# All weight sums of the seven-product windows on VectorE, from plain loads

## The reference

```python
h = h + 0.5 * swiglu(rmsnorm(h, ffn1_norm), w_gate, w_up, w_down)
h = h + mixer(h)                      # retention and differential attention
h = h + 0.5 * swiglu(rmsnorm(h, ffn2_norm), w_gate, w_up, w_down)

def swiglu(x, w_gate, w_up, w_down):
    return (jax.nn.silu(x @ w_gate) * (x @ w_up)) @ w_down
```

## Time and profile before

| | us |
|---|---|
| median of 3 runs | 3177.53 |
| profiled execution | 3177.6 |
| its span, first to last instruction | 3175.9 |
| PE busy | 3056.9 (96%) |
| DVE busy | 2021.3 (64%) |
| ACT busy | 1436.5 (45%) |
| POOL busy | 172.2 (5%) |
| the four stages of windows, about | 4 x 190 |

### The profile page before, as it was taken

The page is one execution under the profiler, slowest core; times in us unless marked ns, Lnnn a source line. Parts: engine busy times, 40 slices in busy tenths (PEclk is TensorE's granted clock), DMA queues, the critical chain, the costliest instruction groups (busy, mean ns, idle before and its releaser), DMA issues.

```text
span 3175.9 us, 55413 instructions
## 1 busy us (share of the span) xinstructions
PE 3056.9 (96%) x20248; PEld 2764.3 (87%) x20248; DVE 2021.3 (64%) x2999; ACT 1436.5 (45%) x2472; POOL 172.2 (5%) x209
## 2 busy tenths in 40 slices
PE   8999998999999899999999999999999999999997
PEld 6778785787887689999899999999999989879986
DVE  4445545773576478855566788647885566768854
ACT  3444433663343255533652455425553365246641
POOL 1000000000000011100000011001110000001100
PEclk9999999999999899999999999999999999999998
DMA  4111232222222247532121377325753212247622
GB/s 154 61 54 60 93 100 87 91 94 93 93 92 93 79 128 184 149 102 91 60 68 54 105 192 179 97 98 150 180 151 100 87 60 68 66 130 187 170 100 99
DMA packets 121787, 341.22 MB, mean 107 GB/s; under 512 B 13774, under 2 KB 13774, under 8 KB 121536
## 3 DMA queue, kind: packets, MB, share of 16 engines
q1 hardware_dynamic: 96768, 290.50, 27.2%
q0 software_dynamic: 23600, 46.87, 8.8%
q10 hardware_dynamic: 1296, 2.14, 0.2%
HBM read 337.29 MB, written 2.17 MB: 107 GB/s over the span
## 4 chain that ended last, share of the span: by engine, by line
PE 66%; issue 24%; DVE 4%; ACT 3%; DMA 2%; DVEq 1%; POOL 1%; ACTq 0%; POOLq 0%; SPq 0%
PE ps L2009 28%; PE ps L2070 9%; PE ps L2300 7%; PE ps L2303 7%; PE ps L2301 7%; PE ps L2585 3%; DMA s_raw<-in_stream 2%; PE ps L2084 1%; DVE rstd L1217 1%; PE ps L2366 1%; PE ps L2152 1%; ACT w_hi L673 1%; ACT f L875 1%; DVE w_lo L1212 1%; DVE h_lo L1223 0%
## 5 line engine op out<-in xcount | busy, mean ns | idle before, releaser
L673 ACT ACTIVATE w_hi<-w_raw 128x1024 fp32r<-128x1024 f32 x352 | 372.7, 1059 | 833.8 <-PE ps L2009 587.4
L1212 DVE TENSOR_TENSOR w_lo<-w_raw,w_hi 128x1024 fp32r<-128x1024 f32 x360 | 440.3, 1223 | 484.6 <-ACT w_hi L673 476.1
L2009 PE MATMUL ps<-f_hi,w_hi 128*128 128x264 f32 (+1 forms) x1488 | 385.7, 317 | 2.0 <-DVE f_lo L1489 2.0
L2009 PE MATMUL ps<-f_lo,w_hi 128*128 128x264 f32 (+1 forms) x1488 | 385.2, 317 | 0.0
L2009 PE MATMUL ps<-f_hi,w_lo 128*128 128x264 f32 (+1 forms) x1488 | 385.1, 316 | 0.0
L2009 PE MATMUL ps<-h_hi,w_hi 128*128 128x512 f32 (+1 forms) x896 | 303.0, 367 | 42.1 <-DVE h_lo L1223 28.5
L2009 PE MATMUL ps<-h_lo,w_hi 128*128 128x512 f32 (+1 forms) x896 | 295.8, 359 | 0.0
L2009 PE MATMUL ps<-h_hi,w_lo 128*128 128x512 f32 (+1 forms) x896 | 294.3, 358 | 0.0
L2009 PEld LDWEIGHTS ps<-f_hi,w_hi 128*128 128x128 f32 x1488 | 244.4, 188 | 22.2 <-issue 2.9
L2009 PEld LDWEIGHTS ps<-f_lo,w_hi 128*128 128x128 f32 x1488 | 245.7, 189 | 19.7
L2009 PEld LDWEIGHTS ps<-f_hi,w_lo 128*128 128x128 f32 x1488 | 245.2, 188 | 19.7
(11 more groups left out here) (365 smaller groups left out, 7489.0 us busy)
## 6 DMA issues: line engine op xcount, KB each, us to landing
w_raw<-in_stream SPq DMA_DIRECT2D x436, 512.0 KB, 3.3
s_raw<-in_stream SPq DMA_DIRECT2D x152, 256.0 KB, 4.9
s_raw<-in_stream POOLq DMA_DIRECT2D x152, 256.0 KB, 4.7
tmp<-in_stream SPq DMA_DIRECT2D x76, 256.0 KB, 5.4
xT<-in_x ACTq DMA_DIRECT2D x8, 256.0 KB, 9.7
xT<-in_x POOLq DMA_DIRECT2D x1, 2048.0 KB, 8.7
out<-tmp SPq DMA_DIRECT2D x8, 256.0 KB, 2.1
const<-in_const POOLq DMA_DIRECT2D x1, 1636.0 KB, 9.2
```

The lines of the kernel that those rows point to most:

```text
L673: nc.scalar.activation(w_hi[:, s, :], w_raw[:, s, :], ACT.Copy).then_inc(hi_done, 1)
L1212: V.tensor_tensor(w_lo[:, s, :], w_raw[:, s, :], w_hi[:, s, :].bitcast(F32), ALU.subtract).then_inc(lo_done, 1)
L2009: last = T.matmul(out[:, p, :], w[:, s, j * P:(j + 1) * P], x[:, k, c0:c1], start=start and j == 0 and r == 0, stop=stop and j == len(ks) ...
```

## The change

SyncE loads w21 (not w22) into s1_raw and no longer loads s3_raw. GpSimd issues no accumulating transfers. DVE's `sums` computes all four sums: s3 from w21 and w11, a drain, s1 in place from w21 and w22 (in tmp), a drain, and s2 and s4 as before. ScalarE waits for DVE's s1 (a new semaphore `s1_sum`) ahead of s1 upper, and no longer waits ahead of s3 upper.

```diff
@@ win_load (SyncE)
-                sp.dma_start(s1_raw[:, q, :], up[:, BLK:]).then_inc(s1_base[q], 16)
-                if not first:
-                    sp.wait_ge(win_lo, 6 * (E - 2) + LO["s3"])
-                sp.dma_start(s3_raw[:, q, :], gate[:, 0:BLK]).then_inc(s3_base[q], 16)
+                sp.dma_start(s1_raw[:, q, :], up[:, 0:BLK]).then_inc(s1_base[q], 16)
@@ GpSimd
-            def win_add(which, L, e, i, q):
-                unit = 2 * (ffn2_base(which, L)[0] + PLAIN + e)
-                w21 = stream_d[at(unit + 1), :, 0:BLK].rearrange("a p n -> (a p) n")
-                pool.wait_ge(s1_base[q], landed(which, L, i, q))
-                pool.sem_inc(carried, 1)
-                pool.dma_start(s1_raw[:, q, :], w21, accum_op=ALU.add).then_inc(s1_in[q], 16)
-                pool.wait_ge(s3_base[q], landed(which, L, i, q))
-                pool.sem_inc(carried, 1)
-                pool.dma_start(s3_raw[:, q, :], w21, accum_op=ALU.add).then_inc(s3_in[q], 16)
...
-                ffn2_sums(0, L)
...
-                ffn2_sums(1, L)
@@ ScalarE
-                def s1_upper(i, q):
-                    act.wait_ge(s1_in[q], landed(which, L, i, q))
+                def s1_upper(E, q):
+                    act.wait_ge(s1_sum, E + 1)
                     nc.scalar.activation(wx_hi[:, 0, :], s1_raw[:, q, :], ACT.Copy).then_inc(win_hi, 1)
...
                 def s3_upper(i, q):
-                    act.wait_ge(s3_in[q], landed(which, L, i, q))
                     nc.scalar.activation(wx_hi[:, 2, :], s3_raw[:, q, :], ACT.Copy).then_inc(win_hi, 1)
@@ VectorE
                 def sums(i, q):
-                    dve.wait_ge(s1_in[q], landed(which, L, i, q))
+                    dve.wait_ge(s1_base[q], landed(which, L, i, q))
                     dve.wait_ge(wg_in[q], landed(which, L, i, q))
+                    dve.wait_ge(w22_in[q], landed(which, L, i, q))
+                    V.tensor_tensor(s3_raw[:, q, :], s1_raw[:, q, :], w_raw[:, q, 0:BLK], ALU.add)
+                    dve.drain()
+                    V.tensor_tensor(s1_raw[:, q, :], s1_raw[:, q, :], tmp[:, 2 + q, 0:BLK], ALU.add).then_inc(s1_sum, 1)
+                    dve.drain()
                     V.tensor_tensor(s2_raw, s1_raw[:, q, :], w_raw[:, q, 0:BLK], ALU.add)
                     dve.drain()
                     V.tensor_tensor(s4_raw, s2_raw, w_raw[:, q, BLK:], ALU.add).then_inc(win_sum, 1)
```

More of the change, by code:

```diff
@@ L294, in program @@
         wg_in, w22_in = [sem("wg_in0"), sem("wg_in1")], [sem("w22_in0"), sem("w22_in1")]
-        s1_base, s1_in = [sem("s1_base0"), sem("s1_base1")], [sem("s1_in0"), sem("s1_in1")]
-        s3_base, s3_in = [sem("s3_base0"), sem("s3_base1")], [sem("s3_in0"), sem("s3_in1")]
+        s1_base = [sem("s1_base0"), sem("s1_base1")]
+        s1_sum = sem("s1_sum")
         win_sum, win_hi, win_lo = sem("win_sum"), sem("win_hi"), sem("win_lo")
@@ L634, in inverse_root @@
                 nc.gpsimd.tensor_tensor(out, out, power[0:out.shape[0], 0:out.shape[1]], ALU.pow).then_inc(done, 1)
-            def win_add(which, L, e, i, q):
-                unit = 2 * (ffn2_base(which, L)[0] + PLAIN + e)
-                w21 = stream_d[at(unit + 1), :, 0:BLK].rearrange("a p n -> (a p) n")
-                pool.wait_ge(s1_base[q], landed(which, L, i, q))
-                pool.sem_inc(carried, 1)
-                pool.dma_start(s1_raw[:, q, :], w21, accum_op=ALU.add).then_inc(s1_in[q], 16)
-                pool.wait_ge(s3_base[q], landed(which, L, i, q))
-                pool.sem_inc(carried, 1)
-                pool.dma_start(s3_raw[:, q, :], w21, accum_op=ALU.add).then_inc(s3_in[q], 16)
-            def ffn2_sums(which, L):
-                win_pairs(pool, lambda e, i, q: win_add(which, L, e, i, q))
-                win_add(which, L, N_WIN - 1, N_WIN // 2, 0)
             for L in range(LAYERS):
-                ffn2_sums(0, L)
                 for k in (0, 1, "m", 2, 3):
@@ L938, in win_pair @@
                     copy_out(by, 3, -1.0)
-                    s1_upper(ni, nq)
+                    s1_upper(E + 1, nq)
                     after(E, "w11")
@@ L996, in ffn2 @@
                 split_hi(*following(u0 + 1, 1))
-                s1_upper(0, 0)
+                s1_upper(E0, 0)
                 act.wait_ge(unit_done, 2 * u0 + 5)
```

## The result

| | before | after |
|---|---|---|
| median, us | 3177.53 | 3193.1 (3191.54 to 3193.62) |
| ratio to before, with its 95% interval | | 1.0053 [1.0038, 1.0067] |
| profiled execution, and its span | 3177.6, 3175.9 | 3193.1, 3191.3 |

The kernel became slower: the medians are 15.6 us apart (0.49%), and the ratio, taken of the means of five runs each, is 1.0053. The forecast was 3200 with a range from 3187 to 3215. So the direction is right, and 7 us of the size are missing. The trace says where.

A forecast was written before the change was run, and what follows sets the result against it. PE set the pace before, and DVE was to become the bound of the window stages. Stage terms of +4.1, +4.6, +6.0 and +7.7 gave +22.4 us on 3177.6, so 3200.0 us, range 3187 to 3215.

The forecast's parts named there:

- DVE's cycle: Window stages: 8.92 us without waits, plus 1.54 for two drained additions and 0.04 for a wait, 10.50 (fourth stage 10.44).
- DVE becomes the bound: Window stages: DVE's 10.50 us cycle passes PE's 10.18, by 0.32 us per window and more in the fourth stage.
- How PE feels it: In most windows PE waits about 0.3 us before its s2 product, because ACT's copy stands behind DVE's s1.
- The gap of 1.67 ahead of the first window: First stage's start: PE's gap of about 2 us goes, since DVE no longer waits for the accumulation.
- Entry: Stage starts: first sum 3.45 us after plain_up, then 18 cycles to the last window, 189.0 us (fourth stage 187.9).
- Third stage: Third window stage: 3.45 us of entry plus 189.0 for 18 cycles of 10.50, so 6.0 us later than before.
- their removal is priced at nothing too: Window stages: POOL's two accumulating transfers per window cost PE nothing, so dropping them was given 0 us.
- Rival 1: Window stages: drains hidden, additions 0.61 us each, cycle 10.14 under PE's 10.18; about 3176 us, chance 0.10.
- Rival 2: Window stages: DVE waits for ACT's upper part of w1, each window 0.3 us longer; 3222 us, chance 0.09.
- Rival 3: Window stages: drain hidden but each addition costs its full 0.69 us, cycle 10.34; 3188 us, chance 0.08.

The follow-up runs named there:

- e3: The changed kernel without the drain between the sums s3 and s1 on DVE; 3181.87 us, ratio to before 1.0018.
- e5: The changed kernel with the sum s3 computed twice, each with its drain, so three additions ahead of s2; 3252.59 us, ratio to before 1.0238.
- e1: The kernel before with only s3 summed on DVE, s1 still from the accumulating transfer; 3170.72 us, ratio 0.9975.
- e2: The kernel before with only s1 summed on DVE (ACT waits for it), s3 still from the accumulating transfer; 3165.51 us, ratio 0.9964.
- e4: The changed kernel, but POOL instead of SyncE issues the plain load of w21; 3194.94 us, ratio to before 1.0058.
- e6: The kernel before plus an unused inverse root (addition, power) on POOL once the windows of stages 1 and 3 are issued; 3166.69 us, ratio 0.9969.
- e8: The kernel before with e2's edit and e6's unused inverse root together; 3160.76 us, ratio to before 0.995.
- e7: From e2, with s3 added on POOL from plain loads instead of an accumulating transfer; 3211.12 us, ratio to before 1.0104.

## Why the prediction was right, and where it was off

1. **DVE's cycle: right.** Forecast 10.50, and 10.44 in the fourth stage; measured 10.50 to 10.51 in the first two and 10.44 in the fourth. The terms hold one by one: 0.77 and 0.78 for the additions, 0.03 for the wait that I put at 0.04. e3 and e5 confirm the drain and the addition by changing each alone.
2. **DVE becomes the bound: right.** e1 and e2 stay at PE's pace, after does not.
3. **How PE feels it: right.** In each steady window of the first two stages PE steps late ahead of s2 by 0.21 to 0.26 us, and in the fourth by 0.41; the step behind it is 0.10 longer than usual. Together that is the window's whole growth (10.18 to 10.50, and 9.92 to 10.44). The gap of 1.67 ahead of the first window is gone.
4. **Entry: right.** The first sum stands 3.45 behind plain_up in stages 1 and 2, as forecast, and 3.44 in the other two. From it to the last lower part of s3 the forecast is 189.0 - 0.93 = 188.07; measured 188.15, 188.13, 189.43, and in the fourth 186.99 for 186.97.
5. **Third stage: off by 1.3 us.** There the cycle alternates between 10.51 and 10.62. Every second window has an idle time on DVE between the sums s3 and s1:

```profile
2229.27 0.70 DVE L1542 TENSOR_TENSOR s_raw<-s_raw,w_raw 128x512 f32<-128x512 f32 x1 [0.28 <-issue]
2230.16 0.69 DVE L1544 TENSOR_TENSOR s_raw<-s_raw,tmp 128x512 f32<-128x512 f32 x1 [0.20 <-issue]
...
2239.90 0.69 DVE L1542 TENSOR_TENSOR s_raw<-s_raw,w_raw 128x512 f32<-128x512 f32 x1 [0.27 <-issue]
```

   The step is 0.89 instead of 0.77. e3, without its drain, has no such step in this stage, but it has one in the second, ahead of the first sum (periods of 10.35 and 10.44 in turn), and e5 has one in the third and fourth (11.28 and 11.38, 11.20 and 11.32). e4, whose DVE code is after's, has it where after has it. So about 0.1 us in every second window goes with the program, and edits move it to another stage or instruction. What it is stays open.

6. **The step that failed: "their removal is priced at nothing too".** I priced POOL's two transfers per window by what they cost PE in the stages, where they cost nothing. Their price stands 200 us later, in the mixer: POOL's first power after them starts late, and DVE waits for it. That term measured -3.10 and -3.90, -7.0 us in all; e6 shows that it can be had without the change. The forecast with it, 3200.0 - 7.0 = 3193.0, is within 0.1 us of the median. That closeness is chance: the stages came 1.5 us longer than forecast, and the rest of the table's outside stretches sum to -1.5.
7. **That rest is a balance of larger pieces, and PE's clock is in several.** At the exit of the second stage DVE reached the first lower part of the down weights 1.39 us sooner behind the cut, mostly since ACT waited 2.13 for those weights where it had waited 3.23. And stretches in which PE's granted clock is 0.50, the lower of its levels of 1.2 and 2.4 GHz, came and went: after has two that before has not, at 1798 and 2170, with 1.5 us each, and lacks some of before's, such as those from 1564 and 2018. Before's own five runs lie 6 us apart, which would fit such pieces coming and going without an edit; no two executions of one kernel have a trace here, so that is not shown.

**The rivals.** Rival 1 (the additions fit) is refuted by the period. Rival 2 (DVE waits for ACT inside its cycle) is refuted: the cycle has no such wait in any stage. Rival 3 (the drain hidden, 3188) needs care. By the total it is nearer than my forecast: 5.1 us below 3193.1, where mine is 6.9 above. By the period it is wrong: 10.34 forecast, 10.51 measured. It gave a fair total by leaving out the wrong term. A total cannot tell two such cases apart; the period can. I also read the sentence quoted from the Trainium skill without the exception that follows it (see e3 above): with the exception it does not lead to rival 3, and my steps of 0.61 were no disagreement.

## What to carry to other kernels

Before work is moved onto an engine, take its cycle from a window in which it waited for nobody, and fill it only up to the pace of the bound. Here one addition was free (and worth 0.3%), the second took the engine past the bound and cost its overshoot in every window. When an engine is relieved, look also at its next work outside the stage; a wait that ends there in "issue" may be its price, and an unused instruction ahead of it may pay it where nobody waits. Then look at the stages again: here that instruction came with a slower pace of PE.

## What the runs showed of the hardware that I had not expected

**A power on POOL is late behind its transfers.** 3.2 to 5.8 us of idle time stand between an addition and the first power after POOL has issued transfers (the unused ones of e6 and e8 included), and at most 0.15 when a power ran 220 us earlier (e6, e8). Without transfers it was 1.65 in the first mixer and at most 0.15 in the second.

**The same wait of PE is followed by a full or by a half clock.** Ahead of the second stage PE waits 3.03 us in before and 3.04 in after, for the same weights. PE's timeline and the granted clock by stretch (the number behind the count in brackets), before:

```profile
1797.80 0.48 PE L2009 MATMUL ps<-h_hi,w_hi 128*128 128x264 f32 x2 [3.03 <-DVE w_lo L1212]
...
1799.07 0.41 PE L2009 MATMUL ps<-h_hi,w_lo 128*128 128x264 f32 x2
1799.32 0.41 PE L2009 MATMUL ps<-h_hi,w_hi 128*128 128x264 f32 x2
```

```profile
1797.60:1799.80 2.20, 2.00 (x16) 1.00 0.45 132
```

and after:

```profile
1796.70 0.48 PE L1994 MATMUL ps<-h_hi,w_hi 128*128 128x264 f32 x2 [3.04 <-DVE w_lo L1192]
...
1798.24 0.64 PE L1994 MATMUL ps<-h_hi,w_lo 128*128 128x264 f32 x2
1798.68 0.64 PE L1994 MATMUL ps<-h_hi,w_hi 128*128 128x264 f32 x2
```

```profile
1797.80:1800.30 2.50, 2.50 (x13) 0.50 0.54 197
```

Two matmuls take 0.25 us from start to start in the one and 0.44 in the other, and DVE's wait for PE grows from 1.99 to 3.53. So here a wait of 3 us on PE cost 1.5 more in one kernel and nothing in the other.

**An addition on POOL is not beside DVE's work.** It took 1.75 us and lengthened a DVE instruction by 1.1 (e7).
